# Rotary rotation of queries and keys: a VectorE product with the neighbouring block of 32 rows in place of a TensorE product with a permutation matrix

## The reference, cut to what matters

```
def apply_rope(x, cos, sin):                       # differential attention, 64 channels
    x1, x2 = jnp.split(x.astype(jnp.float32), 2, axis=-1)
    return jnp.concatenate([x1 * cos - x2 * sin, x1 * sin + x2 * cos], axis=-1).astype(x.dtype)
...
q_l = apply_rope(q_l, cos, sin)                    # q, k: (256 tokens, 8 heads, 2 maps, 64)
k_l = apply_rope(k_l, cos, sin)
...
q_pe = _rope(_rmsnorm(q_pe, qpe_w), cos[None, :, None, :], sin[None, :, None, :])   # 8 heads x 64
k_pe = _rope(_rmsnorm(k_pe, kpe_w), cos[None], sin[None])                           # one, 64
```

## Time and profile before

| | us |
|---|---|
| time, median of 3 runs | 1290.42 (1289.99 to 1291.06) |
| the profiled execution: its own time | 1291.02 |
| the profiled execution: span from first to last instruction | 1289.3 |
| TensorE busy in the span | 1225.1 |
| VectorE busy in the span | 679.0 |
| ScalarE busy in the span | 549.8 |
| mean granted TensorE clock, share of full | 0.984 |

### The profile page before, as it was taken

How to read it: one execution, slowest core, us unless ns; L and a number is a source line. 1 busy time by engine, 2 the same in 40 slices (tenths; PEclk the granted TensorE clock), 3 DMA queues, 4 the chain that set the end, 5 groups by cost and what they waited for, 6 DMA issues and landing times.

```text
span 1289.3 us, 18951 instructions
## 1 busy us (share of the span) xinstructions
PE 1225.1 (95%) x7202; PEld 1002.7 (78%) x7202; DVE 679.0 (53%) x1141; ACT 549.8 (43%) x1026; POOL 87.2 (7%) x124
## 2 busy tenths in 40 slices
PE   7999999999999997999988899999899989999998
PEld 5765787787788885789946899999797675798467
DVE  3444477676433336555196754455664434355743
ACT  3234322222132224544366644444565554466742
POOL 0012011122000001000000200000100000020500
PEclk9999999999999998999989999999999999899899
DMA  9889265678422221323310465554353321363011
GB/s 326 307 309 325 87 196 184 198 263 277 155 98 98 92 87 50 98 77 121 99 34 1 131 196 191 174 184 152 123 179 100 96 89 45 75 201 142 33 43 56
DMA packets 121367, 183.40 MB, mean 142 GB/s; under 512 B 4305, under 2 KB 92672, under 8 KB 121296
## 3 DMA queue, kind: packets, MB, share of 16 engines
q1 hardware_dynamic: 113744, 154.64, 36.2%
q0 software_dynamic: 7552, 27.80, 6.8%
HBM read 181.37 MB, written 1.05 MB: 141 GB/s over the span
## 4 chain that ended last, share of the span: by engine, by line
PE 84%; DVE 7%; ACT 4%; issue 3%; POOL 1%; DMA 0%; DVEq 0%; SPq 0%; ACTq 0%; POOLq 0%
PE ps L440 20%; PE ps L442 20%; PE ps L441 20%; PE ps L751 2%; PE ps L791 2%; PE ps L752 2%; PE ps L753 2%; PE ps L920 2%; PE ps L933 2%; PE ps L1910 1%; PE ps L1954 1%; DVE wl L425 1%; PE ps L2242 1%; PE ps L2244 1%; PE ps L2243 1%
## 5 line engine op out<-in xcount | busy, mean ns | idle before, releaser
L425 DVE TENSOR_TENSOR wl<-raw,wh 128x1024 fp32r<-128x1024 f32 (+2 forms) x242 | 294.8, 1220 | 271.6 <-ACT wh L420 269.1
L440 PE MATMUL ps<-hh,wh 128*128 128x256 f32 (+3 forms) x1256 | 420.8, 335 | 17.1 <-DVE hl L570 11.4
L441 PE MATMUL ps<-hl,wh 128*128 128x256 f32 (+3 forms) x1256 | 412.1, 328 | 0.0
L442 PE MATMUL ps<-hh,wl 128*128 128x256 f32 (+3 forms) x1256 | 411.1, 327 | 0.0
L420 ACT ACTIVATE wh<-raw 128x1024 fp32r<-128x1024 f32 (+2 forms) x242 | 251.9, 1043 | 278.3 <-PE ps L442 256.5
L440 PEld LDWEIGHTS ps<-hh,wh 128*128 128x128 f32 (+1 forms) x1256 | 239.6, 191 | 57.3 <-issue 27.7
L442 PEld LDWEIGHTS ps<-hh,wl 128*128 128x128 f32 (+1 forms) x1256 | 239.7, 191 | 20.8
L441 PEld LDWEIGHTS ps<-hl,wh 128*128 128x128 f32 (+1 forms) x1256 | 238.9, 190 | 21.0 <-issue 0.2
L440 PE MATMUL ps<-ah,wh 128*128 128x256 f32 (+3 forms) x400 | 134.0, 335 | 5.5 <-DVE al L1751 3.0
L441 PE MATMUL ps<-al,wh 128*128 128x256 f32 (+3 forms) x400 | 131.9, 330 | 0.0
L442 PE MATMUL ps<-ah,wl 128*128 128x256 f32 (+3 forms) x400 | 131.7, 329 | 0.0
(11 more groups left out here) (209 smaller groups left out, 1474.8 us busy)
## 6 DMA issues: line engine op xcount, KB each, us to landing
raw<-in_ffn_w_in SPq DMA_DIRECT2D x44, 1024.0 KB, 5.1
raw<-in_ffn_w_out SPq DMA_DIRECT2D x22, 1024.0 KB, 4.9
raw<-in_w_in SPq DMA_DIRECT2D x22, 1024.0 KB, 5.4
big<-in_w_ada SPq DMA_DIRECT2D x16, 1024.0 KB, 9.7
big<-in_w_ada POOLq DMA_DIRECT2D x24, 512.0 KB, 4.4
ex<-in_w_ada POOLq DMA_DIRECT2D x24, 512.0 KB, 5.0
raw<-in_diff_w_in SPq DMA_DIRECT2D x12, 1024.0 KB, 5.1
raw<-in_w_out SPq DMA_DIRECT2D x8, 1024.0 KB, 4.9
```

What stands on the lines that cost most here:

```text
L425: nc.vector.tensor_tensor(split_half(wl, at), raw_half(at)[0], split_half(wh, at).bitcast(F32), ALU.subtract).then_inc(split, 1)
L440: nc.tensor.matmul(o, w_hi, m_hi, start=first, stop=False, **kw)
L441: nc.tensor.matmul(o, w_hi, m_lo, start=False, stop=False, **kw)
L442: return nc.tensor.matmul(o, w_lo, m_hi, start=False, stop=last, **kw)
```

## The change

The permutation matrix, its matmul, its semaphore and its PSUM tiles are gone. VectorE multiplies each block of 32 rows of the scaled tile with the sines of these rows and writes the product to the rows of the neighbouring block in the destination (four instructions for 128 rows, two for 64); then the cosine product into `t1`, then the sum of `t1` and the destination. The sign is in the sine tables. Both inputs of the new products lie on the same rows, the output on others. The only wait inside the rotation is the one behind the cosine product. TensorE's loop has one step less at the end of a list.

```
-    rot = np.zeros((P, P))
-    for m in range(P):
-        if m % 64 < 32:
-            rot[m + 32, m] = -1.0
-        else:
-            rot[m - 32, m] = 1.0
+    turn = np.where(np.arange(P) % 64 < 32, 1.0, -1.0)[:, None]
...
-        "cos_d": np.cos(ang_d), "sin_d": np.sin(ang_d), "cos_m": np.cos(ang_m), "sin_m": np.sin(ang_m),
+        "cos_d": np.cos(ang_d), "sin_d": np.sin(ang_d) * turn, "cos_m": np.cos(ang_m), "sin_m": np.sin(ang_m) * turn,
...
-N_KEPT = 10
+N_KEPT = 9
...
         def units_pe(pe, phase, h_base=None, before=0):
-            for i in range(len(phase) + 2):
+            for i in range(len(phase) + 1):
...
-                if 2 <= i and phase[i - 2].get("rope"):
-                    u = phase[i - 2]
-                    m, w = u["cols"], u["rope"][2]
-                    pe.wait_ge(s_unrm, u["h"] + 1)
-                    positive(pe, s_urdy, u["r"] - 1)
-                    nc.tensor.matmul(ps[0:m, 5 + u["r"] % 2, 0:w], T["rot"][0:m, 0:m],
-                                     nrm[0:m, u["h"] % 2, 0:w], start=True, stop=True).then_inc(s_urot, 1)
...
                     tile = nrm[0:m, u["h"] % 2, 0:w]
+                    for b in range(m // 32):
+                        to, at = slice(32 * b, 32 * b + 32), slice(32 * (b ^ 1), 32 * (b ^ 1) + 32)
+                        mark(nc.vector.tensor_tensor(u["dst"][to], tile[at], T[sin][at, 0:w], ALU.mult))
                     link(nc.vector.tensor_tensor(t1[0:m, 0:w], tile, T[cos][0:m, 0:w], ALU.mult))
-                    dve.wait_ge(s_urot, u["r"] + 1)
-                    link(nc.vector.tensor_tensor(tile, ps[0:m, 5 + u["r"] % 2, 0:w], T[sin][0:m, 0:w],
-                                                 ALU.mult))
-                    nc.vector.tensor_tensor(u["dst"], t1[0:m, 0:w], tile, ALU.add).then_inc(s_urdy, 1)
+                    nc.vector.tensor_tensor(u["dst"], t1[0:m, 0:w], u["dst"], ALU.add).then_inc(s_urdy, 1)
```

More of the change, by code:

```diff
@@ L109, in shape_tables @@
     return {
-        "ident": eye, "ones": np.ones((P, P)), "half": half, "rot": rot,
-        "cos_d": np.cos(ang_d), "sin_d": np.sin(ang_d), "cos_m": np.cos(ang_m), "sin_m": np.sin(ang_m),
+        "ident": eye, "ones": np.ones((P, P)), "half": half,
+        "cos_d": np.cos(ang_d), "sin_d": np.sin(ang_d) * turn, "cos_m": np.cos(ang_m), "sin_m": np.sin(ang_m) * turn,
         "mask": mask, "fold": np.arange(P)[:, None] % 32 == np.arange(8),
@@ L114, in shape_tables @@
     }
-TABLE_COLS = {"ident": P, "ones": P, "fold": 8, "half": P, "rot": P, "cos_d": L, "sin_d": L, "cos_m": L2, "sin_m": L2,
+TABLE_COLS = {"ident": P, "ones": P, "fold": 8, "half": P, "cos_d": L, "sin_d": L, "cos_m": L2, "sin_m": L2,
               "mask": GRID_W, "trig": 2 * L, "dft_c": P, "dft_ns": P, "dft_s": P}
-N_KEPT = 10
+N_KEPT = 9
 ROTARY_AT = sum(list(TABLE_COLS.values())[:list(TABLE_COLS).index("cos_d")])
@@ L364, in build @@
         s_unrm = sem("unit_normed")
-        s_urot = sem("unit_rotated")
         s_ucp = sem("unit_copied")
@@ L832, in units_act, with units_dve @@
                     round_next(act, q)
-        def units_dve(dve, link, phase):
+        def units_dve(dve, link, mark, phase):
             for i in range(len(phase) + 2):
@@ L1844, in _ @@
             dve.wait_ge(s_tab, 16)
-            units_dve(dve, link, DIFF_UNITS)
+            units_dve(dve, link, mark, DIFF_UNITS)
             att_dve(dve, link, mark, ATT["diff"])
@@ L1872, in _ @@
             ffn_out(1, G["ffn1_out"], L, "second")
-            units_dve(dve, link, LAT_UNITS)
+            units_dve(dve, link, mark, LAT_UNITS)
             norm_dve(dve, "lat")
-            units_dve(dve, link, GATE_UNITS)
-            units_dve(dve, link, MLA_UNITS)
+            units_dve(dve, link, mark, GATE_UNITS)
+            units_dve(dve, link, mark, MLA_UNITS)
             att_dve(dve, link, mark, ATT["mla"])
-            units_dve(dve, link, NA_GATE_UNITS)
-            units_dve(dve, link, NA_UNITS)
+            units_dve(dve, link, mark, NA_GATE_UNITS)
+            units_dve(dve, link, mark, NA_UNITS)
             na_dve(dve, mark)
```

## The result

The changed kernel takes 1293.46 us (median of 10 runs, 1291.08 to 1295.40) against 1290.19 for the kernel before (10 runs, 1288.59 to 1292.47). The ratio is 1.0025, 95% interval 1.0015 to 1.0035: slower by 0.25%, more than the 0.2% that a measurement tells from no change. The forecast was 1289.9 and no change. The time lies 0.2 us above the range's upper end, on the side of the rival in which TensorE's clock falls. The profiled execution took 1294.58 with a span of 1292.9 (before: 1291.02 and 1289.3), at a mean granted clock of 0.980 (before: 0.984).

A forecast was written before the change was run, and what follows sets the result against it. TensorE was taken as the bound (95% busy, 84% of the chain that ended last). Places 1, 2 and 3 at +0.1, -0.6 and 0.0 summed to -0.5 us, giving 1289.9 us, no change; range 1286.2 to 1293.3.

The forecast's parts named there:

- the rival in which TensorE's clock falls: Longer TensorE gaps lower its clock: one fall 1291.6 us, chance 0.15; two 1293.3, slower, chance 0.12 for two or more.
- place 1: Differential attention's query and key units, 16 rotations: query stretch loses 2.66 us, key units gain 2.58, net +0.1.
- a query turn: VectorE's work per differential-attention query unit, scaling to scaling: from 2.88 to 4.19 us, above TensorE's 3.27.
- The room of the key units: Differential attention: VectorE idles 3.60 us before a key unit's scaling, which hides 1.3 us of new work.
- Place 3: Second block's eight query parts: rotations become waits, 0.21 to 0.78 and 1.42 to 1.99 us; 0.0 gained of 4.6.
- The last key unit's scaling starts at 571.55, that is 5.11: Differential attention: VectorE's new query turns counted from 5.11 us after the first query unit's start.
- the spacing: VectorE's step from one instruction to the next: 0.42 us per block product, 0.48 for the scaling, without overlap.
- late by 0.9: Differential attention: TensorE's fifth query unit waits for VectorE's scaling, due at 14.49 us instead of 13.51.
- Two or more 0.12: Chance 0.12 that TensorE's clock falls at least twice anew; two falls give 1293.3 us, slower.
- 3.27 busy of 4.19: Argument against clock falls: TensorE in differential attention's query units stays far denser than gaps that led to a fall.
- Each new fall costs 1.7: Price in us of one TensorE clock fall, from 6 us at mean 0.72 of full clock in the old trace.
- Place 2: Second block's shared key, one rotation: TensorE runs without a gap, so -0.6 us; -0.1 if VectorE's cover were gone.

The follow-up runs named there:

- e4: Changed kernel with one in-place product over all rows instead of the block products, exchange of blocks left out: 1284.18 us, ratio 0.9941 to the kernel before.
- e7: Kernel before with block products only for differential attention's first six key units and the shared key, matmuls elsewhere: 1287.40 us, ratio 0.9975.
- e1: Kernel before with block products only in differential attention's 16 units; the second block's nine rotations stay matmuls: 1293.73 us, ratio 1.0025.
- e2: Kernel before with block products only for the second block's shared key and eight query parts: 1293.47 us, ratio 1.0011.
- e6: Changed kernel, differential attention's four block products replaced by four products on whole rows, exchange left out: 1287.76 us in one execution.
- e10: The changed kernel profiled once more, nothing altered: 1291.86 us in one execution.
- e3: Kernel before with block products only for differential attention's eight key units and the shared key; query rotations stay matmuls: 1291.26 us, ratio 0.9990.
- e11: The kernel before profiled once more, nothing altered: 1292.92 us in one execution.
- e9: Kernel before, all rotations by matmul, with only the second block's weight halves rounded and split one step later: 1288.02 us, ratio 0.9963.
- e8: Kernel before with blocks for keys 0-5 and 7, queries 1, 3, 5, 6, 7 and the shared key, plus later second-block weight splits: 1281.35 us, ratio 0.9935.
- e5: Changed kernel with the second block's weight halves rounded and split one step later: 1288.63 us, ratio 0.9991 to the kernel before.

## Why the prediction was wrong, and where it was right

**Right.** TensorE's prices: 0.43 a rotation in place 1 (e4's 6.8 for sixteen, e7's 2.5 for six). That a query turn becomes VectorE's bound at about 4.2 (4.19 forecast, 4.24 measured) and that this gives the key units' gain back. The room of the key units: the idle time before their scaling went from 3.60 to 1.71, and nothing was late. Place 3's waits: 0.78 forecast for 0.21 (0.92 measured), 1.99 for 1.42 (1.98 and 2.04). The slower rival's mechanism and its place.

**Wrong, first: "Place 1: +0.1"**, which was +1.6 in both profiles of after and in e1. The step is "The last key unit's scaling starts at 571.55, that is 5.11". It was read from the old trace, where VectorE had idled 0.87 and waited for ScalarE. After the change VectorE is already the later one: the scaling before stands at 564.96, 1.41 behind the first query unit's start, a key's own turn takes 569.60 - 564.96 = 4.64, and the last key is scaled at 1.41 + 4.64 = 6.05. That is 0.94 more. In the old trace the same two figures are 567.43 - 566.44 = 0.99 and 571.55 - 567.43 = 4.12: 0.42 comes from the rotation that no longer stands between that scaling and the first query unit, 0.52 from the longer turn. I had counted VectorE's new work from the query units on and left it out of the key unit just ahead of them. The second error is the spacing, 0.45 in place of 0.42 and 0.51 in place of 0.48: 8 turns x 0.05 less small change elsewhere, +0.3. Together the third token unit starts at 604.44 - 563.55 = 40.89 instead of 39.63, against 36.97 before, so +3.92 - 2.58 = +1.34. The remaining 0.3 lies in the reading: 563.55, 566.44 and 36.97 are ends of pieces in the chain, 604.44 is the row of a matmul behind a wait. Taken at the second matmul of the first query unit and of the third token unit, before

```profile
566.39 0.28 PE L441 MATMUL ps<-hl,wh 128*128 128x256 f32 x1
...
603.37 0.28 PE L752 MATMUL ps<-wl,hh 128*128 128x256 f32 x1
```

and after

```profile
563.49 0.28 PE L435 MATMUL ps<-hl,wh 128*128 128x256 f32 x1
...
604.66 0.28 PE L746 MATMUL ps<-wl,hh 128*128 128x256 f32 x1
```

the stretch is 36.98 before and 41.17 after, so +4.19 - 2.58 = +1.61, the whole of it. The +1.6 lies within the ends given (-2.8 to +1.7): this is a term mis-sized, with its mechanism right. (The forecast's "late by 0.9" is 14.49 - 13.51 = 0.98 by its own figures; nothing rests on it.)

**Wrong, second: "Place 3: 0.0"** together with "Two or more 0.12". The waits were forecast to 0.15 us, and the trace before already had a fall behind one of two waits of 1.4. Making the same two waits 0.57 longer should have put an extra fall into the likeliest case. By count only one fall is new, which the forecast gave 0.15 and 1.7 us; by cost it is more than its two falls. The argument used against it (3.27 busy of 4.19) is sound but belongs to place 1, where the clock indeed stayed at 1.00; the place at risk was the one where a fall already stood. The price, "Each new fall costs 1.7", was read from a short fall; the second one after cost 2.85 where the old one cost 1.57, and the new first one 3.05. That falls come in such lengths was not in the sum. That the longer waits brought the extra fall is likely, not shown: with block products in place 3 and three splits ahead of the scaling, all four profiles have two falls (after, e2, e6, e10), with the matmul four of five have one (before, e1, e3, e11) and e7 has two. With +1.6 from place 1 and +4.4 from place 3, the last mark of place 3 stands 5.7 us later than before.

**Not forecast, and in the other direction: the rest.** From 1034 us on, after is 2.1 us shorter, though nothing there was changed. The windows of one such stretch, before:

```profile
1114.00:1124.00 10.00, 7.25 (x36) 6.87 (x36) 4.84 (x6) 6.54 (x10) 1.65 (x2) 0.66 0.73 143
```

and after:

```profile
1114.00:1124.00 10.00, 7.25 (x52) 6.49 (x51) 1.22 (x4) 3.19 (x6) 1.65 (x2) 0.95 0.13 31
1124.00:1136.00 12.00, 12.00 (x95) 12.00 (x95) 7.38 (x6) 6.37 (x10) 1.78 (x4) 0.90 1.05 236
```

In 1114 to 1124 the clock is at 0.66 before, with the next 12 us at 1.00; after it is 0.95, then 0.90. As stretch times missing clock that is 10 x 0.34 = 3.4 us before, against 10 x 0.05 + 12 x 0.10 = 1.7 after. Here the fall is the shorter one. After's lag shrinks by 0.9 us across it, and by 0.9 once more near 1194, where the clock in 1190 to 1204 is 0.63 before and 0.79 after. Every profile of a kernel that was changed ahead of this stretch shows -1.9 to -3.7 in the rest, and the second profile of the kernel before 0.0. But both profiles of that kernel have a mean clock of 0.984, and beside e9 its executions at 0.991 took 1287.40 to 1289.71 and those at 0.980 took 1294.90 to 1296.68. So how long the falls are also varies with the execution, and that the change shortens those of the rest isn't shown. The sum in the profiles is +1.6 + 0.3 + 4.4 - 2.1 = +4.2, less 0.6 ahead of place 1 and in the stretches between, +3.6; the medians differ by 3.3.

**Place 2** was forecast at -0.6. In the profiles of kernels with the block product there it is -0.8 four times, -0.4 once and +0.3 four times. The clock sorts them. Over 915 to 952 it is 0.95 on average before, and 0.95 in the four with -0.8 (e2, e6, e8, e10), 0.91 in e3, and 0.86 in the four with +0.3 (after, e4, e5, e7). At the clock of before the term holds, -0.8 for -0.6; a longer fall of the clock, which the forecast didn't count at this place, takes it back. Whether the change brings it is open: after has it and e10, the same kernel, hasn't.

**Left open.** What else, besides its length, decides whether a wait of 1.4 us is followed by a fall. Over the profiles that have such waits: of twelve waits of 1.3 to 1.5 (before, e1, e3, e4, e7, e11) seven were followed by one, of eight waits of 2.0 (after, e2, e6, e10) all eight, and with both waits at 0.4 or less (e5, e8, e9) none of six. That short waits avoid it is shown; that 2.0 is worse than 1.4 is likely from these counts, no more.

## What to carry to other kernels

When work moves to an engine with room, start the count of its new turns in the unit before the crowded stretch, and from that engine's own new schedule, not from a time at which it was idle in the old trace. Several products on changing blocks of rows take their full time plus a gap each on VectorE (here 0.45 for 256 columns, against 0.335 on constant rows); four of them cost more than the matmul of 0.43 that they replace wherever VectorE is near the period, and are free where it idles, so share such work out per unit (e8). Where the trace already has a fall of the clock behind a wait, treat that wait as the first thing that a change may lengthen or remove: rounding and splitting the weights one step later, behind the scaling (e9), was worth 0.37% by itself.

## What the runs showed of the hardware that I had not expected

The granted clock fell to 0.50 behind the same wait of 1.42 us in e7 that left it at 1.00 in the kernel before, in code that is the same; and falls behind alike waits cost between 1.5 and 3.05 us, by how much of the following 24-matmul unit ran at the lower level. The Trainium skill ("TensorE: Matmul & The Clock Gate", A second HAM failure mode) reports a kernel whose frequent short idling made the clock switch back and forth. These profiles agree for two waits of 2.0 in a list of query units, while eight waits of 0.64 to 1.15 at place 1, one in each query unit's turn, left the clock at 1.00.
